# One angle tile for the rope tables of both branches, and attention A begun one block later

## What is computed

```python
h = einsum('bsd,de->bse', x, w_in)
qa, ka, va, gate_a, qb, kb, vb, gate_b, mg_a, mg_b = split(h)
ang = positions[..., None] * 10000 ** (-arange(half) / half)   # half = 32 (A), 64 (B)
out = concat([t1 * cos(ang) - t2 * sin(ang), t2 * cos(ang) + t1 * sin(ang)])   # rope of q, k
o_a = banded_attention(qa, ka, va, 127, sinks)       # 16 heads of 64, 2 kv heads
o_b = three dilated groups (128,1) (512,4) (2048,16) # 12 heads of 128, merged by softmax of lse
y_a = (o_a * silu(gate_a)) @ w_pa;  y_b = (o_b * silu(gate_b)) @ w_pb
merged = sigmoid(mg_a + b0) * y_a + sigmoid(mg_b + b1) * y_b
out = layer_norm(2 ** 0.25 * x + merged @ w_out)
```

## Time and profile before

| | us |
|---|---|
| median of 3 runs | 1463.67 (1462.85 to 1467.24) |
| the profiled execution | 1462.83 |
| its span | 1461.0 |
| TensorE busy | 1412.0 (97%) |
| POOL busy | 651.4 (45%) |
| DVE busy | 488.1 (33%) |
| ACT busy | 487.4 (33%) |
| granted TensorE clock, mean | 0.994 of full |

### The profile page before, as it was taken

One profiled execution on the slowest core, in us unless ns is written; L12 is line 12 of the kernel. 1 busy time (PEld: TensorE's weight loads), 2 busy tenths in 40 slices (PEclk: granted clock), 3 DMA queues, 4 the chain that ended last, 5 costly groups with the idle time before them and its releaser, 6 DMA issues.

```text
span 1461.0 us, 20009 instructions
## 1 busy us (share of the span) xinstructions
PE 1412.0 (97%) x6692; PEld 1184.4 (81%) x6692; DVE 488.1 (33%) x799; ACT 487.4 (33%) x674; POOL 651.4 (45%) x274
## 2 busy tenths in 40 slices
PE   9979899899999999999999999999999999999996
PEld 7858777778978887897888888888888888888885
DVE  5976676772143226104321210110101101301116
ACT  5244454552333333233333322222222222321222
POOL 4423233344534444454543354453454444554446
PEclk9989999999999999999999999999999999999999
DMA  8322222134323233332323243332333423383322
GB/s 256 101 62 69 61 68 62 53 88 115 87 76 102 62 83 86 88 87 79 94 80 98 64 116 87 90 111 72 115 90 96 115 64 108 107 266 102 101 72 116
DMA packets 191674, 140.63 MB, mean 96 GB/s; under 512 B 17296, under 2 KB 179344, under 8 KB 190736
## 3 DMA queue, kind: packets, MB, share of 16 engines
q1 hardware_dynamic: 191632, 140.08, 33.1%
HBM read 135.82 MB, written 4.19 MB: 96 GB/s over the span
## 4 chain that ended last, share of the span: by engine, by line
PE 77%; DVE 14%; ACT 3%; issue 3%; DMA 1%; POOL 1%; SPq 0%; DVEq 0%; POOLq 0%; ACTq 0%
PE acc L975 71%; DVE probs_b L735 2%; PE ps_out L1056 1%; ACT shifted L509 1%; DVE k_b L694 1%; DVE shifted L691 1%; PE ps_turn L1030 1%; PE ps_out L1047 1%; PE ps_scores L999 1%; DVE angle L657 1%; DVE rowmax L708 1%; ACT probs_a L460 1%; DMA raw<-xT 1%; DVE negmax L710 1%; DVE q_a L694 1%
## 5 line engine op out<-in xcount | busy, mean ns | idle before, releaser
L427 POOL TENSOR_TENSOR w_lo<-raw,w_hi 128x1024 fp32r<-128x1024 f32 x260 | 632.3, 2439 | 798.0 <-ACT w_hi L452 784.0
L975 PE MATMUL acc<-x_hi,w_hi 128*128 128x512 f32 x1216 | 480.8, 395 | 0.1
L975 PE MATMUL acc<-x_hi,w_lo 128*128 128x512 f32 x1216 | 474.9, 391 | 0.0
L975 PE MATMUL acc<-x_lo,w_hi 128*128 128x512 f32 x1216 | 474.9, 391 | 0.0
L452 ACT ACTIVATE w_hi<-raw 128x1024 fp32r<-128x1024 f32 x256 | 267.5, 1055 | 440.6 <-PE acc L975 428.7
L975 PEld LDWEIGHTS acc<-x_hi,w_lo 128*128 128x128 f32 x1216 | 228.8, 188 | 48.6
L975 PEld LDWEIGHTS acc<-x_hi,w_hi 128*128 128x128 f32 x1216 | 229.3, 189 | 44.9 <-DVE shifted L691 0.5
L975 PEld LDWEIGHTS acc<-x_lo,w_hi 128*128 128x128 f32 x1216 | 229.3, 189 | 43.6
L975 PE MATMUL acc<-w_hi,x_hi 128*128 128x384 f32 (+1 forms) x512 | 186.3, 364 | 5.3 <-DVE shifted L691 4.7
L975 PE MATMUL acc<-w_hi,x_lo 128*128 128x384 f32 (+1 forms) x512 | 185.3, 362 | 0.0
L975 PE MATMUL acc<-w_lo,x_hi 128*128 128x384 f32 (+1 forms) x512 | 185.2, 362 | 0.0
(11 more groups left out here) (154 smaller groups left out, 1128.3 us busy)
## 6 DMA issues: line engine op xcount, KB each, us to landing
raw<-w_in SPq DMA_DIRECT2D x384, 128.0 KB, 2.3
raw<-w_in SPq DMA_DIRECT2D x256, 96.0 KB, 2.5
raw<-w_out SPq DMA_DIRECT2D x128, 128.0 KB, 3.0
raw<-w_in SPq DMA_DIRECT2D x64, 192.0 KB, 2.7
raw<-w_pa SPq DMA_DIRECT2D x64, 128.0 KB, 2.3
raw<-xT SPq DMA_DIRECT2D x8, 512.0 KB, 5.0
raw<-w_in SPq DMA_DIRECT2D x64, 64.0 KB, 2.2
raw<-w_pb SPq DMA_DIRECT2D x64, 64.0 KB, 2.5
```

The source lines that it names most:

```text
L427: nc.gpsimd.tensor_tensor(dst, raw[:, slot, :], hi.bitcast(F32), ALU.subtract).then_inc(lo_done, 1)
L975: ins = nc.tensor.matmul(into[:, 0:cols], s, m, start=start and k == 0, stop=stop and k == n - 1)
```

## The change

One angle tile serves both branches: its lower 64 partitions carry the 32 frequencies of branch A (twice), its upper 64 the 64 of branch B. DVE computes the two arguments once. ACT writes each table in two activations of 64 partitions, from the half of the argument that belongs to the branch; the sines of A wait for both arguments and stand at block 13 as before, those of B at block 17 instead of 21. The sign of B's sine table is given as a constant. And every start in A's plan is one block later: unit u starts at block 1 + 3u.

```diff
--- before.py
+++ after.py
@@ -97,7 +97,7 @@
     return plan
 
 
-A_PLAN = stages([u * 3 for u in range(A_UNITS)], (2, 3, 5), (3, 5, 6))
+A_PLAN = stages([1 + u * 3 for u in range(A_UNITS)], (2, 3, 5), (3, 5, 6))
 B_PLAN = stages([1 + u * 5 for u in range(B_UNITS)], (3, 4, 7))
 B_PLAN_MERGE = stages([u * 3 for u in range(B_UNITS)], (1, 2, 4))
 
@@ -190,8 +190,7 @@
                           for n, where in (("k_hi_a", 0), ("k_lo_a", 4096)))
 
         angle, turns = (at(n, shared_at + 2048 * k, [P, SEQ]) for k, n in enumerate(("angle", "turns")))
-        rests = [at(f"rest{k}", where, [P, SEQ]) for k, where in
-                 enumerate((shared_at + 2 * 2048, branch_at + 2048, branch_at + 4096, branch_at + 6144))]
+        rest_cos, rest_sin = at("rest_cos", shared_at + 2 * 2048, [P, SEQ]), at("rest_sin", branch_at + 2048, [P, SEQ])
         pos_row = at("pos_row", shared_at + 3 * 2048, [P, SEQ], I32)
         k_rot = at("k_rot", shared_at + 4 * 2048, [P, SEQ])
         vT_a = at("vT_a", shared_at + 5 * 2048, [P, SEQ])
@@ -207,7 +206,7 @@
 
         part_a, part_b = at("part_a", tables_at, [P, 2, SEQ]), at("part_b", tables_at + 4096, [P, 2, SEQ])
         ident = sb("ident", [P, P])
-        rope_col = sb("rope_col", [P, 4])
+        rope_col = sb("rope_col", [P, 2])
         gbias = sb("gbias", [P, 2 * KT])
         sink_row = sb("sink_row", [P, A_HEADS])
         sink_pair = sb("sink_pair", [P, A_HEADS, 2])
@@ -510,12 +509,26 @@
                                                 src[half * (k ^ 1):half * ((k ^ 1) + 1), :], ACT.Copy)
                 last.then_inc(swapped, 1)
 
-            def sines(k):
-
-                table, col = ((cos_a, None), (sin_a, 3), (cos_b, None), (sin_b, 1))[k]
-                act.wait_ge(table_arg, k + 1)
-                scale = 1.0 if col is None else rope_col[:, col:col + 1]
-                nc.scalar.activation(table[:], rests[k][:], ACT.Sin, scale=scale).then_inc(table_done, 1)
+            low_half, high_half = slice(0, P // 2), slice(P // 2, P)
+
+            def sines_a():
+
+                act.wait_ge(table_arg, 2)
+                for rows in (low_half, high_half):
+                    c = nc.scalar.activation(cos_a[rows, :], rest_cos[low_half, :], ACT.Sin)
+                c.then_inc(table_done, 1)
+                for rows in (low_half, high_half):
+                    c = nc.scalar.activation(sin_a[rows, :], rest_sin[low_half, :], ACT.Sin, scale=rope_col[low_half, 1:2])
+                c.then_inc(table_done, 1)
+
+            def sines_b():
+
+                for rows in (low_half, high_half):
+                    c = nc.scalar.activation(cos_b[rows, :], rest_cos[high_half, :], ACT.Sin)
+                c.then_inc(table_done, 1)
+                for rows, sign in ((low_half, -1.0), (high_half, 1.0)):
+                    c = nc.scalar.activation(sin_b[rows, :], rest_sin[high_half, :], ACT.Sin, scale=sign)
+                c.then_inc(table_done, 1)
 
             def iter_a(i, with_attention):
                 for g, (job, _, _, bank, _, last, opens, _) in enumerate(A_BLOCKS):
@@ -525,9 +538,10 @@
                         act.wait_ge(kv_full, 2)
                         nc.scalar.activation(by_block(vT_a[:]), by_residue(ps_out[:]), ACT.Copy).then_inc(v_out, 1)
                         swap_halves(shifted[:], ps_scores[:, 0:SEQ], 32, 0)
-                    if not with_attention and g in (13, 21):
-                        for k in (0, 1) if g == 13 else (2, 3):
-                            sines(k)
+                    if not with_attention and g == 13:
+                        sines_a()
+                    if not with_attention and g == 17:
+                        sines_b()
                     if not with_attention and g == 10:
                         act.wait_ge(v_turned, 1)
                         nc.scalar.activation(twice(v_hi_a), turned_v(), ACT.Copy).then_inc(v_hi_ready, 1)
@@ -667,14 +681,12 @@
             for e in range(8):
                 x_low(e)
             dve.wait_ge(pos_in, 32)
-            for k, (freq, quarter) in enumerate(((2, True), (2, False), (0, True), (0, False))):
-                rest = rests[k]
-                if quarter:
-                    chain(nc.vector.tensor_copy(angle[:], pos_row[:]))
-                    chain(nc.vector.tensor_scalar(angle[:], angle[:], rope_col[:, freq:freq + 1], None, ALU.mult))
-                    reduce_angle(angle[:], angle[:], 65536.0, 0.0)
-                reduce_angle(rest[:], angle[:], 1.0, 0.25 if quarter else 0.0)
-                chain(nc.vector.tensor_scalar(rest[:], rest[:], two_pi / 4 if quarter else 0.0, -pi, ALU.add, ALU.max))
+            chain(nc.vector.tensor_copy(angle[:], pos_row[:]))
+            chain(nc.vector.tensor_scalar(angle[:], angle[:], rope_col[:, 0:1], None, ALU.mult))
+            reduce_angle(angle[:], angle[:], 65536.0, 0.0)
+            for rest, turn in ((rest_cos, 0.25), (rest_sin, 0.0)):
+                reduce_angle(rest[:], angle[:], 1.0, turn)
+                chain(nc.vector.tensor_scalar(rest[:], rest[:], two_pi * turn, -pi, ALU.add, ALU.max))
                 nc.vector.tensor_scalar(rest[:], rest[:], pi, None, ALU.min).then_inc(table_arg, 1)
             dve.wait_ge(small_in, 48)
             nc.vector.tensor_scalar(sink_pair[:, :, 0], sink_row[:], 1.0 / A_SCALE, None, ALU.mult).then_inc(sink_step, 1)
@@ -1185,8 +1197,8 @@
 
 
     p = np.arange(P)
-    rope_rows = np.stack([10000.0 ** (-(p % 64) / 64.0), np.where(p < 64, -1.0, 1.0),
-                          10000.0 ** (-(p % 32) / 32.0), np.where(p % 64 < 32, -1.0, 1.0)], axis=1).astype(np.float32)
+    rope_rows = np.stack([np.where(p < 64, 10000.0 ** (-(p % 32) / 32.0), 10000.0 ** (-(p % 64) / 64.0)),
+                          np.where(p % 64 < 32, -1.0, 1.0)], axis=1).astype(np.float32)
     in_block = (4 * np.arange(32)[None, :] + np.arange(NR)[:, None]).reshape(-1)
     dist = in_block[:, None] - np.concatenate([in_block - P, in_block])[None, :]
     mask_a = np.where((dist >= 0) & (dist < 128), 0.0, MASKED).astype(np.float32)
```

## The result

The changed kernel takes **1473.26 us** (median of 8 runs, 1468.23 to 1475.22), beside 1464.09 for the kernel before in the same comparison (8 runs, 1462.85 to 1467.24): a ratio of 1.0054 [1.0042, 1.0066]. It is slower, where I forecast 1461.1 and a range from 1453 to 1467. Measured again at the end of the study, the same kernel took 1467.58 (8 runs, 1465.07 to 1474.25) beside 1464.44, a ratio of 1.002 [1.0009, 1.003]. So it is slower in both, by 3 and by 9 us, and its runs spread over 10 us (1465.07 to 1475.22 in the two measurements), where those of the kernel before spread over 4.4 here and at most 5.3 later (21 runs). That spread belongs to the explanation.

What follows compares the result with a forecast made beforehand. TensorE, busy 97%, was taken to set the end by its program order. Terms -9.2 + 1.3 + 2.4 + 3.5 - 0.6 = -2.6 us gave 1460.2 by the profile, 1461.1 as median; range 1453 to 1467.

Steps and rivals of the forecast that it cites:

- What bounds it: Whole kernel: TensorE, busy 97%, sets the end by its program order; only its gaps can be won.
- Tables at no cost; first hand-over -9.2: Where attention A's first pass meets the next projection: one angle chain saves DVE 16.2 us, ACT's sines delay nothing; 9.2 gained.
- the clock is part of the price: Old 9 us gap at the first hand-over: TensorE's half level from 82.3 to 92.5 counted in its cost.
- L702's hold and the freed L710: DVE at hand-overs: POOL's pass holds a two-element copy, TensorE waits about 3 us; unit 1's mask loses its 1.83 hold.
- Second and third +0.6 each: Later hand-overs in branch A: gating and og split behind the rope plus copy hold; 0.6 us lost each, 1.3 for two.
- the steady part: Units behind weight roundings start masks late, fewer by one or so: -0.2 us a pass, -0.6 in all.
- Fourth +2.4: Hand-over in branch B's first iteration: weight rounding every three blocks holds DVE again; 2.4 us lost, bounds -1.0 and +3.
- End of the first B iteration +3.5: Unit 7 in branch B: POOL passes hold the tile 2 rope, values 7 at 330.8; 3.5 us lost, bounds 0 and +3.8.
- Sum -2.6 without the clock: All hand-over, B-iteration and steady terms together: 2.6 us gained, to 1461.1, counted as the same.
- rival (b): Clock falls in hand-overs: 10.2 us at half level, one fall 1465.9, two 1470.7; chance 0.1.
- the reading that 3.19 us of idle did not cost the clock: Earlier trace, unit 7's turn in branch B: clock stayed up after 3.19 us idle, though 9.0 us brought it down.
- the sign that the prediction itself had named for (b): New profile: a half level behind one of the gaps, at unit 1's scores or values 7, would show the clock falling.

Runs made afterwards that it cites:

- experiment 5: Changed kernel with idle transposes sized to the gaps: 22 before unit 1's scores, 8 before unit 7's values (30 in B's first iteration); 1462.0 us, ratio 0.9986.
- experiment 1: Changed kernel with A's old plan starts put back, so only the table part is left; 1455.95 us, ratio 0.9941.
- experiment 6: Kernel before with 78 idle transposes in TensorE's 9 us gap at the first hand-over; 1465.25 us, ratio 1.0003.
- experiment 10: Changed kernel with 22 idle transposes ahead of unit 1's scores alone; 1463.54 us, ratio 0.9995.
- 11: Changed kernel measured again with nothing altered; 1467.58 us.
- 4: Kernel before with 140 idle transposes in TensorE's 9 us gap at the first hand-over; 1465.97 us, ratio 1.0013.
- 8: Changed kernel with the old starts for the last pass of branch A alone, inside B's first iteration; 1463.04 us, ratio 0.999.
- 9: Tables-only kernel with ACT's weight rounding of block 0 moved to block 3 and the next to block 5; 1457.05 us, ratio 0.995.
- 3: Changed kernel with idle transposes, too long: 36 before unit 1's scores, 14 before unit 7's values (48 in B's first iteration); 1465.72 us, ratio 1.0008.
- 7: Changed kernel with ACT's weight rounding of block 0 put behind unit 0's exponentials, at block 1; 1465.62 us, ratio 1.0008.

## Why the prediction was wrong

TensorE's place against the kernel before, for the same matmul, worked out from the timelines. The kernel before has the four values of unit 0 at 99.75, 161.05, 222.36 and 283.78, the values of unit 7 at 325.94, and a matmul of branch B, which the plan does not shift, at 371.33. Where the plan has shifted a matmul, 1.37 is added to before's start.

| place | forecast | changed kernel | gaps filled (exp. 5) |
|---|---|---|---|
| values 0, first hand-over | -9.2 | 91.12: -10.0 | 91.21: -9.9 |
| values 0, second | -8.8 | 154.79: -7.6 | 153.74: -8.7 |
| values 0, third | -8.3 | 219.60: -4.1 | 216.04: -7.7 |
| values 0, fourth | -6.1 | 284.55: -0.6 | 279.49: -5.7 |
| values 7 in branch B | -2.6 | 331.74: +4.4 | 326.59: -0.7 |
| branch B, 371.33 before | -2.6 | 378.41: +7.1 | 370.49: -0.8 |

The last column is the waits alone, the distance between the last two columns the clock: 7.9 us at the end, growing by 1.1 (a fall of 3.4 us), 2.5, 1.5 and 2.8 (falls of 6.8 us).

- **What bounds it**: right. TensorE's order set the end.
- **Tables at no cost; first hand-over -9.2**: right. It measured -10.0, and experiment 1 alone -9.5. But the words that the clock is part of the price of the old 9 us gap are wrong: with the clock whole there (experiment 6) the values come only 0.2 us earlier.
- **L702's hold and the freed L710**: right, 2.21 us held to POOL's end. The forecast idle of 3.4 to 4.2 us at unit 1's scores came out at 2.5 to 2.7, while 0.65 to 0.9 stand ahead of block 1. That is a bank wait that I had left out, and so is the 1.03 ahead of the values at 130.88.
- **Second and third +0.6 each**: the size was low. In experiment 5 they are +1.2 and +1.0, where the forecast, with the steady part, has +0.4 and +0.5. ACT's table load now stands behind the wait for og (2.46 us idle, then 1.28 of load), which I had not walked; what it is worth was not tried by itself.
- **Fourth +2.4**: right (+2.0 in experiment 5, +2.2 forecast with the steady part). **End of the first B iteration +3.5**: the mechanism is right, but the size low: +4.9, beyond its bound of 3.8. DVE's rope of tile 2 was caught by POOL as walked (L703 and L706 take 2.60 and 2.64 us from 325.69), and the values of unit 7 wait 3.72.
- **Sum -2.6 without the clock**: experiment 5 is at -2.4 by medians (1462.0, before 1464.44 beside it) and -0.8 by the two spans (1460.2 and 1461.0). The agreement by medians is in part luck, since most runs of the kernel before have some half level that experiment 5 does not have (mean clocks 0.990 to 0.994 against 0.995 to 0.998). By places the terms behind the first hand-over were 2.6 us too small together.
- **The step that failed**: the sum put the clock at nothing. It stands only in rival (b), with a chance of 0.1; what kept it out of the sum was the reading that 3.19 us of idle did not cost the clock. In place of nothing, the clock cost 4.0 us (experiment 10 against 11) to 11.3 us (experiment 5 against the first measurement).
- **Why that reading failed**: it was one execution. The same idle of 3.16 to 3.20 us stands at that place in experiments 1, 4, 6, 8 and 9, and in all five profiled executions 3.4 us at the half level follow it; the kernel before was profiled in an execution where it stayed out. So there was no safe side at 3.19. Nor does one gap's length decide: behind 1.03, 0.91 and 2.56 us, ending within 18 us of each other, the clock falls in the changed kernel, behind 0.64 and 2.5 us at the first hand-over it falls in one execution and not in the other, and behind 1.41 and 1.97 us once in experiment 1. With one filler in the 2.5 us gap, the others alone did not bring it down at a hand-over (experiment 10).
- **The price in rival (b)**: 10.2 us at the half level and 4.8 us for each fall was too much. The falls last 3.4 or 6.8 us and cost 1.1 to 2.8 us each, but there are four or five of them and not one or two. Of the 12.2 us between 1461.1 and the measured 1473.26, 11.3 are the clock by experiment 5; a range that ended at a single fall could not hold them. The half level behind a gap was the sign that the prediction itself had named for (b).

The Trainium skill (TensorE: Matmul & The Clock Gate, What's actually happening) says that throttled is the default and that activity releases it. The runs agree as far as they go: work that is of no use keeps the full clock (experiments 3, 5, 10). I quoted this and then went by the one row of 3.19.

Left open: what exactly in the pattern of gaps decides; why one execution falls four times and another five with the same gaps; and how the shift would do with unit 7's gating kept ahead of the rope, which was not tried.

## What to carry to other kernels

Where TensorE is busy 97%, look at the granted clock behind each group of short idles, and in more than one execution: one trace without a fall does not show that the gap is safe. A rearrangement whose waits come out at about nothing can still lose 4 to 11 us by the clock. Take apart a change of two parts before judging it: here the tables alone give 0.6%, and the shift loses all of it. And a wait caused by a pass on a neighbouring engine was moved here, not removed, by shifting the work around it (experiments 7 and 9).

## Not expected of the hardware

- Behind gaps of 1.03, 0.91 and 2.56 us the clock went from 1.00 to 0.50, with TensorE busy all of 150 to 153. Behind 3.19 us in the earlier trace rows it did not, but behind the same idle (3.16 to 3.20 us) in five other profiled executions it did.
- The number and length of the falls differ from execution to execution (23.9 and 34.2 us at the half level). The mean clock of the runs goes with it, and so does a spread of 10 us for one kernel; with the gaps filled it is 2.6.
- A copy of two elements on DVE was held 2.21 and 2.37 us, to the end of POOL's weight pass. The Trainium skill (GPSIMD Engine Reference, Specifications) names as held the instructions of a two-port mode or with two SBUF inputs. The copy has one input, so of the two only the first could cover it; no run here shows the mode.
